# Leaving out the identity transposes that fill TensorE's waits in the router of a hybrid decoder trunk

## The reference

```python
def moe_swiglu(h, w_router, w1, w3, w2):
    ...
    logits = jnp.dot(xf.astype(F32), w_router.astype(F32))
    top_logit, top_e = lax.top_k(logits, TOP_K)
    gates = jax.nn.softmax(top_logit, axis=-1)
    ...
    def expert_block(args):
        xb, e = args
        return (jax.nn.silu(xb @ w1[e]) * (xb @ w3[e])) @ w2[e]
```

## Time and profile before

| | |
|---|---|
| time, median of 3 runs | 2060.63 us (2059.93 to 2060.92) |
| time of the profiled execution | 2059.9 us |
| its span, first to last instruction | 2058.2 us |
| PE busy | 1979.8 us, 96% of the span |
| PEld / DVE / ACT / POOL busy | 85% / 76% / 54% / 4% |
| mean granted TensorE clock | 0.990 of full speed |
| router, from the logits to the first expert product | 802.7 to 829.2 us |
| L595 transposes | 88, of them 58 in the router |

### The profile page before, as it was taken

One profiled execution on the slowest core, in us unless ns is written; L12 is line 12 of the kernel. 1 busy time (PEld: TensorE's weight loads), 2 busy tenths in 40 slices (PEclk: granted clock), 3 DMA queues, 4 the chain that ended last, 5 costly groups with the idle time before them and its releaser, 6 DMA issues.

```text
span 2058.2 us, 34371 instructions
## 1 busy us (share of the span) xinstructions
PE 1979.8 (96%) x12246; PEld 1755.2 (85%) x12247; DVE 1567.9 (76%) x1964; ACT 1101.3 (54%) x1269; POOL 91.3 (4%) x104
## 2 busy tenths in 40 slices
PE   7999999999989999999999999999999999999993
PEld 6889887878779788999999988788999888999882
DVE  6866535353567586888888899998888998888996
ACT  5532433232335423555655577777555776555773
POOL 0000000000000001200100010100000101000101
PEclk9999999999999999999999999999999999999997
DMA  5312623232322214777777799999777999776983
GB/s 196 103 62 93 259 89 102 82 102 82 112 72 83 76 58 151 258 245 258 269 244 267 251 362 373 363 377 358 263 260 245 335 378 334 252 266 236 378 318 145
DMA packets 218812, 450.44 MB, mean 219 GB/s; under 512 B 13217, under 2 KB 64433, under 8 KB 218769
## 3 DMA queue, kind: packets, MB, share of 16 engines
q1 hardware_dynamic: 210416, 421.05, 58.6%
q0 software_dynamic: 8352, 28.80, 3.7%
HBM read 432.23 MB, written 17.58 MB: 219 GB/s over the span
## 4 chain that ended last, share of the span: by engine, by line
PE 83%; DVE 10%; issue 3%; ACT 2%; DMA 1%; DVEq 0%; POOL 0%; ACTq 0%; SPq 0%; POOLq 0%
PE ps L583 18%; PE ps L585 17%; PE ps L584 17%; PE ps L925 12%; PE ps L942 8%; PE ps L927 5%; PE ps L944 3%; DVE w_lo L1777 2%; DVE w_lo L1774 1%; PE ps L652 1%; ACT w_hi L1189 1%; DVE ex L1356 1%; DVE w_lo L1331 1%; PE ps L846 1%; ACT w_hi L1191 0%
## 5 line engine op out<-in xcount | busy, mean ns | idle before, releaser
L1774 DVE TENSOR_TENSOR w_lo<-raw,w_hi 128x1024 fp32r<-128x1024 f32 x340 | 415.4, 1222 | 81.4 <-ACT w_hi L1189 78.9
L925 PE MATMUL ps<-xt,w_hi 128*128 128x304 f32 x1792 | 457.1, 345 | 2.7 <-DVE xt L1788 2.3
L927 PE MATMUL ps<-xt,w_lo 128*128 128x152 f32 x1792 | 420.0, 234 | 0.0
L1189 ACT ACTIVATE w_hi<-raw 128x1024 fp32r<-128x1024 f32 x340 | 357.5, 1052 | 107.6 <-PE ps L927 56.9
L1777 DVE TENSOR_TENSOR w_lo<-raw,w_hi 128x1024 fp32r<-128x1024 f32 x340 | 415.0, 1221 | 0.0
L1191 ACT ACTIVATE w_hi<-raw 128x1024 fp32r<-128x1024 f32 x340 | 356.3, 1048 | 0.0
L927 PEld LDWEIGHTS ps<-xt,w_lo 128*128 128x128 f32 x1792 | 343.0, 191 | 0.1
L925 PEld LDWEIGHTS ps<-xt,w_hi 128*128 128x128 f32 x1792 | 338.8, 189 | 3.3 <-issue 3.2
L583 PE MATMUL ps<-act_hi,w_hi 128*128 128x512 f32 x608 | 242.0, 398 | 5.5 <-DVE act_lo L1375 5.5
L585 PE MATMUL ps<-act_hi,w_lo 128*128 128x512 f32 x608 | 239.9, 395 | 0.0
L584 PE MATMUL ps<-act_lo,w_hi 128*128 128x512 f32 x608 | 239.8, 394 | 0.0
(11 more groups left out here) (330 smaller groups left out, 3164.8 us busy)
## 6 DMA issues: line engine op xcount, KB each, us to landing
raw<-in_moe_w_dram SPq DMA_DIRECT2D x672, 512.0 KB, 5.2
raw<-in_w_in_dram SPq DMA_DIRECT2D x19, 1024.0 KB, 5.1
raw<-in_ffn_w_gate_dram SPq DMA_DIRECT2D x11, 1024.0 KB, 5.4
raw<-in_ffn_w_up_dram SPq DMA_DIRECT2D x11, 1024.0 KB, 5.3
raw<-in_ffn_w_down_dram SPq DMA_DIRECT2D x11, 1024.0 KB, 4.9
raw<-in_w_out_dram SPq DMA_DIRECT2D x8, 1024.0 KB, 4.9
y_rows<-mult POOLq DMA_DIRECT2D x1, 8192.0 KB, 29.5
y_rows<-yacc POOLq DMA_DIRECT2D x8, 512.0 KB, 5.2
```

The source lines that it names most:

```text
L925: pe.matmul(pairs_of(ps[:, bank, 0:2 * NW]), hi_[:, k % 4, f * P:(f + 1) * P], xt[:, k, :, 0:NW], start=k == 0, stop=False)
L927: last = pe.matmul(ps[:, bank, NW:2 * NW], lo_[:, k % 4, f * P:(f + 1) * P], xt[:, k, 0, 0:NW], start=False, stop=k == KT - 1)
L1189: act.activation(slot_hi[p % 6][:, 0:half], raw6(p)[:, 0:half], ACT.Copy).then_inc(w_hi_half, 1)
L1774: dve.tensor_tensor(slot_lo[p % 6][:, 0:half], raw6(p)[:, 0:half], f32(slot_hi[p % 6][:, 0:half]), ALU.subtract)
```

## The change

The four calls of `spin` in the router are left out. The calls in `norm_transposes` stay, as do all waits, all products and every other engine's program. The transposes' target (bank 7 of PSUM) isn't read before a later product overwrites it, so what is computed is the same.

```diff
             last.then_inc(logits_turned, 1)
-            spin(ps[:, 7, 0:P], 7)
             pe.wait_ge(logits_copied, 1)
...
             last.then_inc(logits_done, 1)
-            spin(ps[:, 7, 0:P], 24)
             pe.wait_ge(route_ready, 1)
...
                 pe.sem_inc(t_done, 2 * EC)
 
-            spin(ps[:, 7, 0:P], 13)
             pe.wait_ge(pick_ready, 1)
...
                     last.then_inc(xt_tr, 1)
 
-            spin(ps[:, 7, 0:P], 14)
             turned_next = pe.alloc_register("pe_turned_next")
             pe.wait_ge(items_ready, 1)
```

## The result

The changed kernel took 2069.47 us (median of 9 runs, 2062.64 to 2073.34) against 2060.63 (9 runs, 2058.79 to 2062.64) of the kernel before on the same chip: a ratio of 1.0041, 95% interval 1.0028 to 1.0054. It is slower, by 8.8 us in the medians. The profiled execution took 2072.64 us, with a span of 2071.0; of the 88 transposes of L595 the 30 in the norms are left.

A forecast was written before the change was run, and what follows sets the result against it. It took TensorE's big products to bound the kernel, with DVE leading in the router. Terms 0 + 0.1 + 0 + 0 = +0.1 us on the profiled 2059.9, with the median 0.7 higher, gave 2060.7 us, range 2058.8 to 2063.8.

The forecast's parts named there:

- What bounds the kernel: Whole kernel: the chain is 83% PE and 10% DVE; in the router PE's short products wait for DVE four times.
- the premise: Router: the transposes hold TensorE's full clock, so without them it falls; a full clock without them would prove this wrong.
- What their absence leaves: Router: PE idles 0.7, 3.0, 2.35 and up to 3.8 us; the clock falls around 813 and returns in the pick.
- Price of a cold rank product: Router's ten rank records at half clock: 0.9 us more, mostly covered by DVE's weight split; term 0.1, bounds 0 and 0.3.
- Price of a cold pick product: Router's 64 pick records: end 1.4 to 2.8 us late, covered by 2.66 us; term 0, bounds 0 and 0.1.
- The start of the experts: First expert products: PE idles the same 2.3 us, the half-clock dip at 830.7 stays as it is; term 0.
- the rival of a longer dip: First expert products: half clock for 6.7 us instead of 3.4, 1.3 more lost, 0.3 hidden; 2061.6 to 2062.5, chance 0.16.
- The rival of a dip that goes away: First expert products: the dip at 830.7 vanishes, giving back at most 0.3 us; 2060.4 us, chance 0.07.
- What the removed work frees: Router's four transpose groups: each ends before the wait behind it does; term 0, gain at most 0.05 us.
- The slow rival: Router: half clock through the whole pick product, +4.7 us in all, 2065.3 us; chance 0.05.
- the signs for right: 30 L595 records; half clock about 811 to 821; pick's end 1.4 us later; L1783 at 827.5; first expert product at 829.2.
- the signs for wrong: Full router clock; DVE idle ahead of its reads or L1788 released by ACT after 828.5; more DVE or ACT idle, 835–867.

The follow-up runs named there:

- d1_late_pick: The kernel before with 45 transposes instead of 13 ahead of the pick product: 2064.51 us, ratio 1.0021.
- s1_pad: The changed kernel with 116 more TensorE instructions, nearly all never run, so that the code behind keeps its old place: 2064.14 us, ratio 1.0019.
- d2_no_scatter: The changed kernel, code place restored by padding, with GpSimd's eight scatters held until the first item's split rows are ready: 2061.17 us, ratio 0.9997.
- f1_drop14: The kernel before without only the last group of 14 transposes, code place kept by padding: 2060.43 us, ratio 1.0006.
- g3_hold_only: The changed kernel, code place not restored, with GpSimd's eight scatters held until the first item's split rows are ready: 2065.40 us, ratio 1.0028.
- s2_shift: The kernel before, all transposes kept, with 140 more TensorE instructions, nearly all never run, that shift its code: 2065.31 us, ratio 1.0025.
- r1_pad: The changed kernel with 116 semaphore increments executed at the start of TensorE's program to restore the code's place: 2074.05 us, ratio 1.0076.
- r2_shift: The kernel before, all transposes kept, with 140 semaphore increments executed at the start of TensorE's program: 2077.84 us, ratio 1.0089.

## Why the prediction was wrong

I forecast 2060.7 us, within 2058.8 to 2063.8, and gave "slower" 0.05. The kernel took 2069.47.

- *What bounds the kernel* and the premise: right. The transposes hold the clock. In `d1_late_pick` it stays full over 90 transposes in the router, and without the 24 it falls. For these float32 transposes this contradicts, again, the rule of the Trainium skill (TensorE: Matmul & The Clock Gate, Part 4: PE-mode transpose), by which the change would have left the clock as it was.
- *What their absence leaves*: right in kind. The clock fell in the wait for the routing and came back within the pick, as forecast. It was at half for 10.2 us, 814.4 to 824.6, which less the 3.06 us by which the router begins later is 811.3 to 821.5: the stretch that I gave as a sign (811 to 821). The sum didn't use that stretch. It charged the pick with a dip of 3.3 or 6.7 us, and neither row was as long as this one.
- *Price of a cold rank product*: right. Ten records took 1.04 us more (forecast 0.9); DVE read them 818.65 − 817.34 = 1.31 us after it began the second half of the weight split, 1.14 before: 0.17 us lost (forecast 0.1, bounds 0 and 0.3).
- *Price of a cold pick product*: this is the step that failed. The delay itself was inside the bounds, though its parts differ from mine: 4.5 us of the half clock lay in the pick, whose first 16 records took 4.21 us, 0.26 each against 0.13 at full clock, so twice and not 1.7 times as long. The pick took 10.73 us (820.10 to 830.83) instead of 8.53 (816.85 to 825.38), 2.2 late, where the cover was 2.66. With the scatters held, that cover is just what the runs show: R is 26.55 in both kernels. The sum took for granted that ACT is released when the pick ends. It is, in the earlier trace rows; but 2.2 us later eight scatters of GpSimd are under way, and the release comes up to 5 us after the end. I named DVE's and ACT's work as cover and never looked at GpSimd's row in that stretch. The term I put at 0 to 0.1 is +3.6 us (`s1_pad`), of which the hold takes away 3.0 (`d2_no_scatter`).
- *The start of the experts*: I left the dip at 3.3 us; it was 6.7, behind 5.45 us of idle time. So the rival of a longer dip came true as a mechanism, at a lower price than its 1.3 less 0.3 us: from the first expert product to the second item's, less the idle time at the branch, it is 178.1 us against 177.6, so 0.5 (and 0.6 in `f1_drop14`). The rival of a dip that goes away came true in four kernels, `g3_hold_only` among them, and gave nothing back.
- *What the removed work frees*: its time, nothing, was right, but it missed a term. Leaving out instructions also moves all code behind them. The wait at the branch is 3.83 − 0.37 = 3.5 us longer, the half clock behind it is 15 products in 3.20 us against 101 in 12.30, 15 × (0.213 − 0.122) = 1.4: 4.9 of the 5.7 us behind the first expert product. Of the other 0.8 the longer dip has 0.5; some 0.3 is left, over 1018 us behind the second item's gate and up products in which the kernels differ by 1.0. The shift alone costs 4.7 in the medians (`s2_shift`). No part of my sum had a place for it; it is more than half of the result.
- *The slow rival* gave 2065.3 by a half clock through the whole pick. It named the right side, with another mechanism: the clock was full again 6.2 us before the pick ended.
- Of the signs for right, three appeared: 30 records of L595, the half clock at its place, full again before the pick's end, and DVE's first subtraction where I said (830.73 − 3.06 = 827.67). The pick's end and the first expert product were later than I said. Of the signs for wrong, one appeared as written, that of a wrong cover: the second subtraction of DVE (L1788, now L1784) released by ACT, later than 828.5.

## What to carry to other kernels

Cover that you compute from one engine's end to the next engine's start holds only at the moment where the trace shows it. When an edit moves that moment, look at what every other engine, GpSimd's DMA issues too, has under way at the new one. And an edit that adds or removes instructions ahead of a runtime loop can move the branch to a worse place: compare with a version whose code keeps its place (padding that never runs) before the time is put down to what was removed, since here that part alone was +4.7 us.

## What was not expected of the hardware

- **A late increment behind scatters.** The release that follows TensorE's last product came 1.4 to 4.95 us after the modelled end whenever the end fell 6.4 us or more behind the first of eight scatters that followed one another, with at least five begun, and within 0.2 us at 5.4 us with four begun, with no scatter going out, or 2.7 us after the fourth when the rest were held. ACT is the only engine that waits for it, so the runs don't tell whether it leaves TensorE late or reaches ACT late. ACT's own increment to DVE took 0.04 us in `r1_pad` (836.49 + 0.42 to 836.95), with one scatter still to come. The Trainium skill (Perfetto Trace Analysis, Tensor Engine Instruction) notes that the end of a matmul in a trace is modelled and that the semaphore is pushed after the acknowledgement of PSUM. That leaves room for such a gap, but names no link to GpSimd. The path that the two share is open: no run here shows it. Open too is the rest of `s1_pad`: of its 3.6 us the hold removes 3.0, and the other 0.6 lies within the spread of these comparisons.
- **The wait at a branch goes by the place of the code**: 0.3 to 0.4 us in the kernel before and in all whose loop is shifted by 0, 64 or 256 instructions, 3.3 to 3.8 in the four with shifts of −116 and +140 (the change, `g3_hold_only`, `r2_shift`, `s2_shift`), with a half clock of 3.2 us behind it in the two whose clock is shown above.
- **Semaphore increments that TensorE executes cost 0.15 us each**: the first product came at 14.56 us behind 88 of them, 18.81 behind 116 and 22.49 behind 140, (22.49 − 14.56) / 52 = 0.15.
